# Decoder layer on one core: biases of all experts loaded once, expert weights in half transfers over a nine-slot ring

## What is computed

```python
g = jnp.minimum(xb @ w_gate[e] + b_gate[e], SWIGLU_LIMIT)
u = jnp.clip(xb @ w_up[e] + b_up[e], -SWIGLU_LIMIT, SWIGLU_LIMIT)
act = g * jax.nn.sigmoid(SWIGLU_ALPHA * g) * (u + 1.0)
out = act @ w_down[e] + b_down[e]
return y.at[rows].add(out * wts[:, None].astype(out.dtype))
```

## Time and profile before

| | |
|---|---|
| median of 3 runs | 1293.62 us (1293.12 to 1296.02) |
| the profiled execution's own time | 1294.46 us |
| its span in the profile | 1292.7 us |
| PE busy | 1171.6 us, 91% of the span |
| PEld, DVE, ACT, POOL busy | 577.3, 471.5, 268.8, 20.8 us |
| moved by DMA | 459.03 MB, mean 355 GB/s over the span |
| transfer rate from about 390 us on | 426 to 429 GB/s in nearly every slice |

### The profile page before, as it was taken

How to read it: one execution, slowest core, us unless ns; L and a number is a source line. 1 busy time by engine, 2 the same in 40 slices (tenths; PEclk the granted TensorE clock), 3 DMA queues, 4 the chain that set the end, 5 groups by cost and what they waited for, 6 DMA issues and landing times.

```text
span 1292.7 us, 14002 instructions
## 1 busy us (share of the span) xinstructions
PE 1171.6 (91%) x5380; PEld 577.3 (45%) x5380; DVE 471.5 (36%) x815; ACT 268.8 (21%) x409; POOL 20.8 (2%) x29
## 2 busy tenths in 40 slices
PE   6898999997889999999999999989898989989897
PEld 5686787775644333433334333333333232323332
DVE  6679878874531312222222221213121212212131
ACT  4544555542111020101102010110201020001100
POOL 0200000010000000000000000000000000000000
PEclk9998999997989999999999999999999999999999
DMA  8544464376659999999999999999999999999995
GB/s 287 207 148 150 137 217 163 131 286 227 259 244 427 424 428 427 429 426 428 428 428 426 429 426 428 428 426 428 427 428 427 429 426 428 426 426 428 427 428 208
DMA packets 59833, 459.03 MB, mean 355 GB/s; under 512 B 9440, under 2 KB 10080, under 8 KB 35232
## 3 DMA queue, kind: packets, MB, share of 16 engines
q1 hardware_dynamic: 57520, 454.70, 85.3%
q0 software_dynamic: 1104, 3.93, 1.0%
q10 hardware_dynamic: 1184, 0.07, 0.1%
HBM read 457.64 MB, written 1.05 MB: 355 GB/s over the span
## 4 chain that ended last, share of the span: by engine, by line
PE 56%; DMA 26%; DVE 11%; issue 3%; ACT 3%; DVEq 0%; ACTq 0%
PE bank L1508 27%; DMA experts_ring<-in_w_up 22%; PE bank L1266 12%; PE bank L1558 8%; DVE ring_split L788 3%; DMA experts_ring<-in_w_down 3%; PE bank L1496 3%; PE bank L1526 3%; PE bank L1513 2%; PE bank L1235 1%; DVE region L1186 1%; DVE region L1210 1%; DMA small<-in_g_mix 1%; DMA ring<-in_w_in 1%; ACT region L758 1%
## 5 line engine op out<-in xcount | busy, mean ns | idle before, releaser
L1508 PE MATMUL bank<-experts_ring,region 128*64 128x512 f32 x2048 | 457.0, 596 | 15.4 <-DVE region L1195 12.5
L1508 PEld LDWEIGHTS bank<-experts_ring,region 128*64 128x64 f32 x2048 | 141.1, 137 | 298.7 <-issue 281.9
L1558 PE MATMUL bank<-experts_ring,region 128*64 128x512 f32 x1024 | 230.5, 597 | 42.9 <-ACT region L758 25.1
L1266 PE MATMUL bank<-ring_split,region_split 128*128 128x512 f32 x768 | 235.2, 408 | 20.8 <-DVE ring_split L788 11.1
L1266 PEld LDWEIGHTS bank<-ring_split,region_split 128*128 128x128 f32 x768 | 147.8, 196 | 56.0 <-DVE ring_split L788 12.7
L1558 PEld LDWEIGHTS bank<-experts_ring,region 128*64 128x64 f32 x1024 | 74.0, 137 | 178.9 <-issue 113.6
L1266 PE MATMUL bank<-ring_split 128*128 128x512 f32 x288 | 114.4, 397 | 0.0
L1220 DVE COPY region<-bank 64x512 f32<-64x512 f32 x32 | 22.2, 694 | 252.3 <-PE bank L1558 252.3
L788 DVE TENSOR_TENSOR ring_split<-ring,ring_split 128x2048 fp32r<-128x2048 f32 x42 | 95.7, 2288 | 0.3
L1203 DVE TENSOR_SCALAR region<-bank 128x512 f32<-128x512 f32 x32 | 22.1, 691 | 195.2 <-PE bank L1513 195.2
L541 ACT ACTIVATE ring_split<-ring 128x2048 fp32r<-128x2048 f32 x42 | 80.1, 1911 | 39.7 <-DMA ring<-in_w_out 16.5
(11 more groups left out here) (166 smaller groups left out, 599.2 us busy)
## 6 DMA issues: line engine op xcount, KB each, us to landing
experts_ring<-in_w_gate SPq DMA_DIRECT2D x64, 2048.0 KB, 33.3
experts_ring<-in_w_up SPq DMA_DIRECT2D x64, 2048.0 KB, 33.4
experts_ring<-in_w_down SPq DMA_DIRECT2D x64, 2048.0 KB, 33.1
ring<-in_w_in SPq DMA_DIRECT2D x28, 1024.0 KB, 5.2
ring<-in_w_mem_kv SPq DMA_DIRECT2D x4, 1024.0 KB, 9.5
ring<-in_w_b_attn SPq DMA_DIRECT2D x4, 1024.0 KB, 5.1
ring<-in_w_out SPq DMA_DIRECT2D x4, 1024.0 KB, 5.0
region<-in_b_gates POOLq DMA_DIRECT2D x6, 512.0 KB, 4.9
```

Source lines behind the costliest of these rows:

```text
L1266: ins = nc.tensor.matmul(UB[u % 3][:, :], a[:, k, toks], b[:, cols], start=(k == 0 and m == 0), stop=(k == k_n - 1 and m == 2))
L1508: ins = nc.tensor.matmul(dst[h * SLOTS:(h + 1) * SLOTS, :], XE[:, kk, e * SLOTS:(e + 1) * SLOTS], w[:, k, h * HALF:(h + 1) * HALF], start= ...
L1558: ins = nc.tensor.matmul(bank[2][h * SLOTS:(h + 1) * SLOTS, :], AHT[:, k, half * SLOTS:(half + 1) * SLOTS], w[:, k, h * HALF:(h + 1) * HAL ...
```

## The change

It does five things.

- A piece is loaded in two transfers, each 128 partitions by 8 KB. Each slot has two landing semaphores; PE waits for the second in the middle of the piece. A new semaphore `half_used`, raised by PE after the first half, releases the first half of the slot, `used` the second.
- The slot table is a plain ring of nine for a turn's pieces 0 to 17, and takes slots 1 to 6 of that order again for pieces 18 to 23. So the slot of a turn's piece was last held by the piece 9 before it (pieces 9 to 17), 8 before it (18 to 23), 7 before it (1 to 6) or 15 before it (0, 7 and 8).
- The biases of all 32 experts are loaded once, as 128 rows of 512 floats in two transfers; ACT makes the upper part and DVE the lower part once, both before the expert loop, at the end of the mixer.
- For each pair DVE copies four columns per map of the identity into `BIAS_PICK`, each spread over 64 columns; PE multiplies the 128 upper rows and then the 128 lower rows by this selector, which makes two bias matmuls for one.
- The constant table loses the 512 columns of the old selector, and the copy and clearing of L1168 and L1169 go.

```diff
-BY_TWELVE = {0: 8, 4: 0, 8: 7}
-BY_EIGHT = {1: 5, 2: 4, 3: 6, 5: 2, 6: 1, 7: 3}
-TURN_SLOT = [BY_TWELVE[q % 12] if q % 4 == 0 else BY_EIGHT[q % 8] for q in range(PER_TURN)]
+MOE_SLOT = (8, 5, 4, 6, 0, 2, 1, 3, 7)
+TURN_SLOT = [MOE_SLOT[q % RING] for q in range(2 * RING)] + [MOE_SLOT[q] for q in range(1, 7)]
...
-                sp.dma_start(dst, part).then_inc(ring_in[moe_slot(q)], 16)
...
+                for c in range(2):
+                    if turn is not None:
+                        sp.wait_ge((half_used, used)[c], place_left(turn, q))
+                    sp.dma_start(dst[:, 2 * c:2 * c + 2, :], part[:, 2 * c:2 * c + 2, :]).then_inc(ring_in[moe_slot(q)][c], 16)
+
+            def biases():
+                for m, b in enumerate((b_gate, b_up)):
+                    sp.dma_start(BIAS[m * 2 * EXPERTS:(m + 1) * 2 * EXPERTS, :], b.rearrange("e (h n) -> (e h) n", h=2)
+                                 ).then_inc(bias_in, 16)
...
+            act.wait_ge(bias_in, 32)
+            nc.scalar.activation(BIAS_UP, BIAS, ACT.Copy).then_inc(bias_upper, 1)
...
-                        act.wait_ge(bias_in, it * 64 + 64)
-                        for first in (0, BIAS_LOW):
-                            nc.scalar.activation(BIAS_R[first:first + BIAS_ROWS, :], BIAS[s][first:first + BIAS_ROWS, :],
-                                                 ACT.Copy).then_inc(bias_upper, 1)
...
+            dve.wait_ge(bias_upper, 1)
+            nc.vector.tensor_tensor(BIAS_LOW, BIAS, BIAS_UP, ALU.subtract).then_inc(bias_lower, 1)
...
-            nc.vector.tensor_copy(SEL_R, con[0:BIAS_K, C_SEL:C_SEL + BIAS_ROWS * SLOTS]).then_inc(sel_ready, 1)
-            nc.vector.memset(BIAS_R.bitcast(F32), 0.0).then_inc(bias_cleared, 1)
...
-                        dve.wait_ge(bias_upper, it * 2 + 2)
-                        low = slice(BIAS_LOW, BIAS_K)
-                        nc.vector.tensor_tensor(BIAS_R[low, :], BIAS[s][low, :], BIAS_R[low, :], ALU.subtract).then_inc(bias_lower, 1)
                         dve.wait_ge(slots_free, it + 1)
                         build_slots(i * 2 + 2)
+                        rows_of_pair = ident.rearrange("p (m r) -> p m r", m=2)[:, :, bass.ds(i * 4, 4)]
+                        nc.vector.tensor_copy(BIAS_PICK.rearrange("p (m r s) -> p m r s", m=2, r=4),
+                                              rows_of_pair.unsqueeze(3).to_broadcast([P, 2, 4, SLOTS])).then_inc(bias_pick_built, 1)
...
-                    pe.wait_ge(ring_in[moe_slot(q)], moe_landed(turn, q))
...
+                        if k % 2 == 0:
+                            pe.wait_ge(ring_in[moe_slot(q)][k // 2], moe_landed(turn, q))
...
+                        if k == 1:
+                            ins.then_inc(half_used, 1)
...
-                pe.wait_ge(bias_lower, it + 1)
-                nc.tensor.matmul(dst[:, :], sel[:, 2 * m + e, :], BIAS_R, start=False, stop=True).then_inc(used, 1)
+                pe.wait_ge(bias_pick_built, it + 1)
+                pick = BIAS_PICK[:, (2 * m + e) * P:(2 * m + e + 1) * P]
+                nc.tensor.matmul(dst[:, :], pick, BIAS_UP, start=False, stop=False)
+                nc.tensor.matmul(dst[:, :], pick, BIAS_LOW, start=False, stop=True).then_inc(used, 1)
```

More of the change, by code:

```diff
@@ L87 @@
             _at[_u] = _H
[L90 to L93, removed]
+C_ID, C_TRI, C_MASK, C_IOTA, C_COS, C_SIN, C_NSIN, C_ONE = 0, 128, 256, 512, 640, 704, 768, 832
+C_ALL = 960
 def constants():
@@ L108, in constants @@
         c[:, base:base + NT * HD // 2] = table.reshape(NT, P, HD // 2).transpose(1, 0, 2).reshape(P, -1)
-    sel = (np.arange(BIAS_ROWS)[:, None, None] == np.arange(BIAS_ROWS)[None, :, None]) * np.ones((1, 1, SLOTS))
-    for first in (0, BIAS_LOW):
-        c[first:first + BIAS_ROWS, C_SEL:C_SEL + BIAS_ROWS * SLOTS] = sel.reshape(BIAS_ROWS, -1)
     c[:, C_ONE:C_ONE + P] = 1.0
@@ L235, in decoder_layer @@
         PWT = region[7][:, 512:768]
[L236 to L239, removed]
+        BIAS = region[7][:, 1024:1536]
+        BIAS_UP = region_r[7][:, 1536:2048]
+        BIAS_LOW = region_r[6][:, 1536:2048]
+        BIAS_PICK = region_r[3][:, 0:512]
         bank = [ctx.enter_context(nc.psum_tensor(f"bank{i}", [P, HALF], F32)) for i in range(8)]
@@ L250, in decoder_layer @@
         oT_split, mgT_split = sem("oT_split"), sem("mgT_split")
-        ring_in = [sem(f"ring_in{i}") for i in range(RING)]
+        ring_in = [[sem(f"ring_in{i}_{h}") for h in range(2)] for i in range(RING)]
+        half_used = sem("half_used")
         gbias_in = [sem(f"gbias_in{i}") for i in range(3)]
@@ L280, in decoder_layer @@
         bias_in, used = sem("bias_in"), sem("used")
-        bias_cleared, sel_ready, bias_upper, bias_lower = (sem(n) for n in ("bias_cleared", "sel_ready", "bias_upper", "bias_lower"))
+        bias_pick_built, bias_upper, bias_lower = (sem(n) for n in ("bias_pick_built", "bias_upper", "bias_lower"))
         g_read, sig_done, gs_done, u_read = (sem(n) for n in ("g_read", "sig_done", "gs_done", "u_read"))
@@ L383, in _, with load_expert @@
             load(4)
-            def load_expert(pair, q):
+            def load_expert(pair, q, turn=None):
                 j = q % PER_PAIR
@@ L392, in load_expert @@
                 dst = moe_ring[:, moe_slot(q), :].rearrange("p (k n) -> p k n", k=4)
-                sp.dma_start(dst, part).then_inc(ring_in[moe_slot(q)], 16)
[L395 to L400, removed]
+                for c in range(2):
[6 more added lines that the diff above has]
+                                 ).then_inc(bias_in, 16)
             def rest_of_turn(turn, d):
                 for q in range(RING, PER_TURN):
[L404 to L407, removed]
+                    load_expert(d * 2 + q // PER_PAIR, q, turn)
             def start_of_turn(turn, d):
                 for q in range(RING):
[L411 to L414, removed]
+                    load_expert(d * 2, q, turn)
             for H in range(HALVES, 2 * N0):
@@ L428, in _ @@
                     sp.wait_ge(unit_done, UNIT_OF[("ga1", NT - 1, 0)] + 1)
-                    biases(0, 0)
+                    biases()
                     load_expert(0, 1)
@@ L1484, in _ @@
             pe.wait_ge(rounds_ready, 1)
-            pe.wait_ge(sel_ready, 1)
+            pe.wait_ge(bias_lower, 1)
             n_rounds = pe.value_load(rounds[0:1, 0:1], min_val=1, max_val=SEQ // SLOTS)
```

2 lines of the change are left out of this document (removed).

## The result

The changed kernel takes 1297.87 us (median of 19 runs, 1296.05 to 1299.62) against 1294.90 us for the kernel before (19 runs on the same chips, 1293.09 to 1296.14). The ratio is 1.0023, with a 95% interval of 1.0016 to 1.0030: 3.0 us slower. The forecast was 2.8 us slower, 1296.4, against the median of the three runs known then. The profiled execution took 1297.48 us, with a span of 1295.6.

The account below looks back on a forecast made before the run. The expert loop was taken as bound by its stream of weights through DMA; start -6.3, packets +14.6, biases -8.4, holes +4.7 and tail -1.8 summed to +2.8 us, 1296.4 us against the median; the forecast's own range was 1293 to 1300.5.

Parts of the forecast that it names:

- start of the stream: Expert loads: piece 9's first half, waiting only for half of piece 0, is issued at 366.6 us: -6.3 us.
- biases out of the stream: Expert stream: without four-row bias transfers burdening a few DMA engines, a piece takes 4.905 us, not 4.951: -8.4 us.
- packets: Expert stream: halves make 8 KB packets, eight more per engine at 10 ns each, 0.080 us a piece: +14.6 us.
- holes: Early expert pairs: stream waits for slots at pieces 20 and 25, 2.1 and 2.6 us: +4.7 us.
- tail: After the last landing: PE has four matmuls left in place of eight: -1.8 us.
- The 0.6 us of an earlier loop start: Part of the start term: loop begins 0.6 us earlier as DVE's L1168 and L1169 go, counted from 0.9 us.
- The choice of 10 ns: Packets term: fixed cost per packet read from 2 and 4 KB rows; other fits gave 7.2 and 11.4 ns.
- a rate of 427.6 GB/s for the stream without biases: Biases term: pace assumed once the bias transfers leave the expert stream, 4.905 us a piece.
- At nothing: Items counted as zero: bias load and splits, DVE's selector copy (4 us cover), PE's waits, SP's issues, smaller table load.

Follow-up runs that it names:

- a1_once_only: Changed kernel with the old slots and whole pieces, keeping the biases loaded once and the selector with two bias matmuls: 1286.95 us, ratio 0.9932 to the kernel before.
- a3_old_table: Changed kernel with the old slot table alone, half transfers, half release and biases as changed: ratio 1.0022 to the kernel before.
- a4_by_partition: Changed kernel with whole-piece release, new slots, each piece as two transfers of 64 adjacent partitions, 16 KB packets: 2180.21 us, ratio 1.683 to the kernel before.
- d1_spread_rows: Changed kernel plus one sixteen-row bias transfer at each pair's border, into every eighth partition: 1299.69 us, ratio 1.0037 to the kernel before.
- b2b_four_rows_back: Changed kernel with the four four-row bias transfers put back between pairs, into a buffer no longer read: 1305.55 us, ratio 1.0076 to the kernel before.
- b5_every_other: Changed kernel with whole-piece release, new slots, each piece as two transfers of even and odd partitions, 16 KB packets: ratio 0.9943 to the kernel before.
- b4_one_bias_matmul: Changed kernel without the second bias matmul of each projection, lower parts of gate and up biases left out: 1295.88 us, ratio 1.0005 to the kernel before.

## Why the prediction was right

The time, its sign and its size came out, and so did the five terms, none further off than about 1 us. The runs split the stretch from the issue of piece 9 to PE's start on the last piece or half. It is 907.99 us before, 899.51 in a1_once_only (373.74 to 1273.25), 915.22 in a3_old_table (369.42 to 1284.64) and 918.84 in the changed kernel (366.67 to 1285.51). Piece 9's issue in a1_once_only:

```profile
373.74 0.36 SPq L392 DMA_DIRECT2D experts_ring<-in_w_down  x1
```

| term | forecast | measured |
|---|---|---|
| start of the stream | -6.3 | -6.2 |
| biases out of the stream | -8.4 | -8.5 (a1_once_only against before) |
| packets, with what else the halves cost | +14.6 | +15.7 (a3_old_table against a1_once_only) |
| holes | +4.7 | +3.6 (changed kernel against a3_old_table); 4.0 by the rate |
| tail | -1.8 | -1.7 |
| sum | +2.8 | +2.9 |

Start, stretch and tail add up to the difference of the spans (1295.6 - 1292.7) by themselves; what the runs add is the split of the middle. The numbers of a run are from one trace each. The medians agree: a1_once_only is 8.1 us faster than before, and a3_old_table has the time of the changed kernel.

- **The start** was right: issue at 366.67 for 366.6. Half a piece of PE's work and the issue took 2.15 us from PE's start at 364.52, 2.07 forecast. The 0.6 us of an earlier loop start are luck, though. a1_once_only has the same savings on DVE and starts its loop at 365.76, later than before (365.13), and among the other kernels of this text with the changed kernel's mixer (without a4_by_partition, which loads at half rate) it lies between 362.3 (d1_spread_rows) and 366.7 us (b2b_four_rows_back).
- **Packets** were right: (59.66 - 58.72) / 12 = 0.078 us a piece against a1_once_only, 0.080 forecast, 14.3 us in all. The choice of 10 ns from the rows of 2 and 4 KB holds at 8 KB and again at 4 KB (9.9 and 9.3 ns). The rule of the Trainium skill ("DMA: Bandwidth & Descriptors", "Why small descriptors are slow (HBM only)"), 3 cycles or an estimated 3.5 ns, doesn't agree with these runs; the measurement decides. The 2 us per transfer of the same page's fit (section "Anatomy of one DMA — SWDGE (gpsimd) path", where it is given for that path) don't show in this full queue either: b5_every_other doubled the transfers for nothing that shows. The halves cost 1.3 us more that no term had, at the very end: the last pair takes 1285.51 - 1224.57 = 60.94 us in the changed kernel and 1284.64 - 1223.92 = 60.72 in a3_old_table, where the others take 59.66; in a1_once_only it takes no longer than the rest. b5_every_other, with whole packets in two transfers, has it too (60.15 us for the last pair by its landings, 58.73 for the others), so it seems to go with two transfers a piece. Why is open.
- **Biases out of the stream** was right in size, and the reason given, a few slow engines, is shown by the four engines that end last. The step took the late pace (4.951 us) for the whole stream, and a rate of 427.6 GB/s for the stream without biases. The late pairs alone would give 0.69 / 12 = 0.058 us a piece, 10.5 us; the whole stretch is 8.5 shorter, since the early pairs lose less (by its landings pair 2 of the kernel before takes 58.9 us, pair 3 59.3, the later ones 59.4). So two errors offset each other: the stream without biases runs at 4.893 us a piece and not 4.905, and the one with them was taken too slow over the whole. The reason isn't complete: one packet on each engine, none of them burdened more than another, cost 0.34 us a pair and not 0.09.
- **Holes** were at their places. They go with the new table, since a3_old_table has none, and PE's second bias matmul makes them longer (b4_one_bias_matmul, 1.6 us less). They were forecast about 1 us too long.
- **The tail** was right: 10.1 us for 11.8, -1.7.
- **At nothing** was right for the selector, done 5 us early, and for SP, if not for the reason given (below). The smaller table and the one bias load lie before the loop, where the starts scatter by 4.4 us; no run shows them.

So the mechanism held. The close hit of 0.2 us is luck all the same: packets with their end cost 1.1 us more than forecast, holes 1.1 less, and a loop start somewhere else in its scatter would have moved the trace by more.

## What to carry to other kernels

Where a queue of transfers is the bound and is never empty, its price is read per packet: cutting a transfer for finer release pays only if the tail and the start gain more than the packets cost over the whole stream, here 3.5 us against 16. Small transfers in such a stream cost far more than their bytes, here 8.5 us in the launch for 32 KB a pair, and belong before it. The mean rate doesn't show this where a few engines carry them; compare when the first and the last engine finish a transfer. And an earlier start of a stream is worth nothing if the consumer can't free the ring in time: look for the first place where it runs dry before counting the gain.

## What the runs showed of the hardware

- **Four rows, four engines.** Four transfers of four 2 KB rows a pair left the rate at 428 GB/s but kept only a quarter of the engines busy (share 0.25 and 0.22) from 8 to 3 us before the last landing, and made the stream 8.5 us longer (7.4 in b2b_four_rows_back).
- **Adjacent partitions.** A transfer of 16 KB rows into 64 adjacent partitions of SBUF ran at 216 GB/s with a DMA share of 1.01; into every other partition, or into all 128, at 428. For sixteen rows of 2 KB the price was 0.34 us a pair adjacent and 0.18 spread.
- **SP's queue fills.** Issuing one expert transfer took SP 0.33 us before. In the changed kernel, from its instructions by line (duration in ns, min/median/max):

```profile
L392 SPq DMA_DIRECT2D experts_ring<-in_w_gate x128: 328/1927/6297, 267.9 to 1227.7; - x128
L392 SPq DMA_DIRECT2D experts_ring<-in_w_up x128: 327/379/2136, 307.1 to 1236.4; - x128
L392 SPq DMA_DIRECT2D experts_ring<-in_w_down x128: 328/1919/6292, 350.4 to 1256.3; - x128
```

  SP stands in the issue itself, which is why its line comes up in the chain. The time to landing is 26 us with halves (10 transfers of 2.49 us) and 15.3 us with quarters (12 of 1.28 us), while whole pieces with 7 (33 us before) or 5 (25 us in a1_once_only) never met the limit. So the queue seems to take ten to twelve transfers of this kind. It cost nothing here, as ten of them are still 26 us of work.
